# Who issues the weight loads, and who scales the last tile's gate, in a fused HGRN2 and pooling step on one core

## The reference

```
h = rmsnorm(x, norm_g);  z = h @ w_in          # q f i g_a u g_b m_a m_b
fgate = lb + (1 - lb) * sigmoid(f);  kin = 1 - fgate
o, S  = hgrn2(silu(q) * 128**-0.5, kin, i, log(fgate), S0)   # 4 heads of 128, chunks of 32
y_a = (rmsnorm(o) * silu(g_a)) @ w_proj_a
y_b = (mixed_pool(u) * pool_scale * silu(g_b)) @ w_proj_b
out = x + (sigmoid(m_a) * y_a + sigmoid(m_b) * y_b) @ w_out;  y = rmsnorm(out, final_norm_g)
```

## Time and profile before

| | us |
|---|---|
| median of 3 runs | 1368.67 |
| lowest, highest | 1368.1, 1369.56 |
| the profiled execution's own time | 1367.73 |
| its span, first to last instruction | 1366.0 |
| granted TensorE clock over the span | 0.999 |

### The profile page before, as it was taken

How to read it: one execution, slowest core, us unless ns; L and a number is a source line. 1 busy time by engine, 2 the same in 40 slices (tenths; PEclk the granted TensorE clock), 3 DMA queues, 4 the chain that set the end, 5 groups by cost and what they waited for, 6 DMA issues and landing times.

```text
span 1366.0 us, 21237 instructions
## 1 busy us (share of the span) xinstructions
PE 1351.6 (99%) x8236; PEld 1338.2 (98%) x8236; DVE 921.5 (67%) x1637; ACT 684.0 (50%) x994; POOL 248.6 (18%) x218
## 2 busy tenths in 40 slices
PE   9999999999999999999999999999999999999997
PEld 8999999999999999999999999999999999999997
DVE  8999655669974455698744467986545689974443
ACT  7556434355664344565643345665434456653332
POOL 3004131110132211101222020112310200140001
PEclk9999999999999999999999999999999999999999
DMA  6543633346526333565353335644433366634327
GB/s 219 152 129 123 217 117 115 115 122 206 148 94 223 123 108 109 147 179 149 113 204 122 108 124 152 174 134 151 167 122 108 125 175 200 177 112 172 122 95 81
DMA packets 140692, 195.92 MB, mean 143 GB/s; under 512 B 83760, under 2 KB 100656, under 8 KB 138928
## 3 DMA queue, kind: packets, MB, share of 16 engines
q1 hardware_dynamic: 140448, 194.54, 46.8%
q10 hardware_dynamic: 144, 0.01, 0.0%
HBM read 174.91 MB, written 19.61 MB: 142 GB/s over the span
## 4 chain that ended last, share of the span: by engine, by line
PE 86%; DVE 10%; DMA 1%; issue 1%; ACT 1%; SPq 0%; DVEq 0%; ACTq 0%
PE Z L551 27%; PE Z L553 27%; PE Z L552 27%; DVE wlo L1095 2%; PE B L604 1%; PE B L682 1%; PE B L672 1%; DVE h_b L1147 1%; DVE kj L1199 0%; DVE xres L1505 0%; DVE snew L1268 0%; DMA vtm<-v_blocks 0%; PE B L581 0%; DMA wraw<-w_all 0%; ACT hhi L1050 0%
## 5 line engine op out<-in xcount | busy, mean ns | idle before, releaser
L1095 DVE TENSOR_TENSOR wlo<-wraw,whi 128x1024 fp32r<-128x1024 f32 x278 | 362.8, 1305 | 306.5 <-ACT whi L823 306.5
L551 PE MATMUL Z<-hhi,whi 128*128 128x416 f32 x1576 | 552.5, 351 | 0.0
L553 PE MATMUL Z<-hhi,wlo 128*128 128x416 f32 x1576 | 549.3, 349 | 0.0
L552 PE MATMUL Z<-hlo,whi 128*128 128x416 f32 x1576 | 549.2, 348 | 0.0
L823 ACT ACTIVATE whi<-wraw 128x1024 fp32r<-128x1024 f32 x278 | 293.3, 1056 | 413.4 <-PE Z L553 412.3
L551 PEld LDWEIGHTS Z<-hhi,whi 128*128 128x128 f32 x1576 | 296.0, 188 | 0.9 <-issue 0.8
L552 PEld LDWEIGHTS Z<-hlo,whi 128*128 128x128 f32 x1576 | 296.0, 188 | 0.5
L553 PEld LDWEIGHTS Z<-hhi,wlo 128*128 128x128 f32 x1576 | 295.9, 188 | 0.3
L553 PE MATMUL Z<-mhi,wlo 128*128 128x416 f32 x320 | 112.3, 351 | 0.0
L552 PE MATMUL Z<-mlo,whi 128*128 128x416 f32 x320 | 111.8, 349 | 0.0
L551 PE MATMUL Z<-mhi,whi 128*128 128x416 f32 x320 | 111.5, 348 | 0.0
(11 more groups left out here) (243 smaller groups left out, 1642.0 us busy)
## 6 DMA issues: line engine op xcount, KB each, us to landing
wraw<-w_all SPq DMA_DIRECT2D x278, 512.0 KB, 3.5
xin<-xT SPq DMA_DIRECT2D x4, 1664.0 KB, 8.3
yT<-xres SPq DMA_DIRECT2D x4, 1664.0 KB, 8.5
xres<-xT SPq DMA_DIRECT2D x4, 1664.0 KB, 7.3
v_blocks<-h_vt SPq DMA_DIRECT2D x80, 52.0 KB, 3.1
vtm<-v_blocks SPq DMA_DIRECT2D x20, 192.0 KB, 3.9
ktm<-k_blocks SPq DMA_DIRECT2D x20, 192.0 KB, 3.5
k_blocks<-kt SPq DMA_DIRECT2D x64, 52.0 KB, 1.9
```

The costliest lines, as they stand in the source:

```text
L551: pe.matmul(out, wh, xh, start=first, stop=False)
L552: pe.matmul(out, wh, xl, start=False, stop=False)
L553: return pe.matmul(out, wl, xh, start=False, stop=final)
L1095: dve.tensor_tensor(wlo[n % RING][:], raw(t, n)[:], whi[n % RING][:].bitcast(F32), ALU.subtract).then_inc(wlo_made, 1)
```

## The change

Two things move to ScalarE. In tile 4 only, `kin` is made there from `sf` (one activation with a scale and a bias of one value for each partition), and the second half of `vms` is made there in slot 4h+8, as four activations of 96 x 128 scaled by a mask column each; the vector engine keeps the first half. The two halves get a semaphore each, and the clearing of `vms` goes (TensorE reads 96 rows only). In all tiles, from unit 12 of tile 0 on, ScalarE issues the loads of raw weights: at the end of its slot s it waits until `wlo` of unit s+2 is made, then issues the load of unit s+5 on its own DMA queue. SyncE keeps the loads of slots 3 to 11 of tile 0 and all other transfers.

```diff
+SYNC_LOADS = 12
 # SyncE
-                    if (s + RAW < NU or not last) and not (first(t) and (s + RAW < FIRST or s == 8)):
+                    if first(t) and FIRST <= s + RAW and s < SYNC_LOADS and s != 8:
                         weights(t, s)
 # SyncE, values_in
-                    sp.wait_ge(vms_made, 2 * h)
+                    for made in vms_made:
+                        sp.wait_ge(made, h)
 # TensorE
-                            pe.wait_ge(vms_made, 2 * h + 1)
+                            pe.wait_ge(vms_made[0], h + 1)
...
-                        pe.wait_ge(vms_made, 2 * h + 2)
+                        pe.wait_ge(vms_made[1], h + 1)
 # ScalarE
+            def weights(t, n):
+                act.wait_ge(wlo_made, nth(t, NU, n))
+                r = (t * NU + n) % RAW
+                act.dma_start(wraw[r][:], w_all[(n + RAW) % NU]).then_inc(w_landed[r], 16)
...
                         if s == 4 * h + 1:
                             sigmoid(t, "f", h, sf[h % 2], z_sem("f", h))
+                            if last:
+                                if h >= 2:
+                                    act.wait_ge(k_made, nth(t, 2 * H, 2 * (h - 2) + 1))
+                                else:
+                                    act.wait_ge(k_made, nth(t - 1, 2 * H, 2 * (h + 2) + 1))
+                                act.wait_ge(z_sem("f", h), z_done(t, "f", h))
+                                act.activation(kin[h % 2][:], sf[h % 2][:], ACT.Identity, bias=oml[:, h:h + 1],
+                                               scale=noml[:, h:h + 1]).then_inc(kin_made, 1)
...
+                        if s == 4 * h + 8 and last:
+                            act.wait_ge(split_v, 2 * h + 2)
+                            act.wait_ge(smasks, SMASKS)
+                            n = 3 * SAMPLE
+                            for b in range(4):
+                                ins = act.activation(vms[1][0:n, b, :], vs[h // 2][0:n].bitcast(F32), ACT.Copy,
+                                                     scale=bmask[0:n, 4 + b:5 + b])
+                            ins.then_inc(vms_made[1], 1)
...
+                if not (first(t) and s + 2 < SYNC_LOADS) and (s + 2 + RAW < NU or not last):
+                    weights(t, s + 2)
 # the vector engine
-                    if s == 2 and last:
-                        for v in vms:
-                            dve.memset(v[:].bitcast(F32), 0.0)
...
-                        if s == 4 * h + 1:
+                        if s == 4 * h + 1 and not last:
                             dve.wait_ge(z_sem("f", h), z_done(t, "f", h))
...
-                                for half in range(2):
-                                    dve.tensor_tensor(
-                                        vms[half][0:n], v[0:n].bitcast(F32).unsqueeze(1).broadcast_to([n, 4, P]),
-                                        bmask[0:n, 4 * half:4 * half + 4].unsqueeze(2).broadcast_to([n, 4, P]),
-                                        ALU.mult).then_inc(vms_made, 1)
+                                dve.tensor_tensor(
+                                    vms[0][0:n], v[0:n].bitcast(F32).unsqueeze(1).broadcast_to([n, 4, P]),
+                                    bmask[0:n, 0:4].unsqueeze(2).broadcast_to([n, 4, P]),
+                                    ALU.mult).then_inc(vms_made[0], 1)
```

More of the change, by code:

```diff
@@ L305, in step_kernel @@
         hist_kept, ybm_made, mlo_made = sem("hist_kept"), sem("ybm_made"), sem("mlo_made")
-        h32_made, hlo_made, y_made, vms_made = sem("h32_made"), sem("hlo_made"), sem("y_made"), sem("vms_made")
+        h32_made, hlo_made, y_made, vms_made = sem("h32_made"), sem("hlo_made"), sem("y_made"), [sem(f"vms_made{i}") for i in range(2)]
         lb_made, zeroed, ptmp_made = sem("lb_made"), sem("zeroed"), sem("ptmp_made")
```

## The result

The changed kernel takes 1373.0 us (median of six runs, 1371.97 to 1375.5), the kernel before, run beside it, 1368.8 us. The ratio is 1.0035 with a 95% interval of 1.0025 to 1.0044: slower by 4.2 us, by the medians, where 2.5 us less was forecast. The profiled execution is the slowest of the six: its own time is 1375.5 us for a span of 1373.8.

What follows compares the result with a forecast made beforehand. TensorE, busy 99% of the span, was taken as the bound, so only its waits could go: 2.3 us in tile 4 plus 0.4 in tile 0, less 0.2, is 2.5 off 1368.67, giving 1366.2 us; range 1365.0 to 1368.9.

Steps and rivals of the forecast that it cites:

- the loads, on SyncE's queue: In slot 4h+8, without the block's issue ahead of them, `vtm` and `ktm` are asked for 0.6 us earlier in every head.
- the slower rival: Late raw blocks make the scores miss TensorE in the heads of tiles 1 to 3: 1372.2 to 1374.7 us; chance 0.12.
- Tile 4 gives back 2.3 us: In tile 4's heads, relieving the vector engine removes TensorE's waits: 1.82 us idle plus 0.51 in matmul ends.
- 0.2 for ScalarE: Taken off the gain for ScalarE's new work showing in tile 4's thin margins; bounds nothing and 0.77 us.
- Tile 0 gives back 0.4: In tile 0, the earlier request for `ktm` covers TensorE's 0.38 us wait for it.
- ScalarE's new work: In tile 4, four `vms` instructions take 1.1 us and `kin` 0.52 to 0.65 per head, with 0.2 us showing.
- 265 issues at 0.35 us each: Load issues on ScalarE over all tiles: 93 us, hidden; `whi` to `whi` at a tile's end becomes 4.68 us.
- The new waits: 0: ScalarE's waits for `wlo` of unit s+2 cost 0; a block 1.7 us late stalls some tenths, within the margin.

Runs made afterwards that it cites:

- the block behind the trip: All loads on SyncE, gate and `vms` on ScalarE; against that kernel, slot 4h+8's block is issued behind the loads of `vtm` and `ktm`: 1366.03 us.
- the kernel with small blocks: The changed kernel, but each load ScalarE issues fetches only 64 of the block's 1024 columns: 1365.99 us, ratio 0.9982.
- the paced one: The changed kernel, but SyncE still waits for the `wlo` of each slot, though it issues no block there: 1377.56 us, ratio 1.0067.
- the block ahead of the stores: All loads on SyncE, gate and `vms` on ScalarE; against that kernel, slot 4h+8's block goes before the keys' stores in tiles 1 to 4: 1368.33 us.

## Why the prediction was wrong, by its steps

**The step that failed is "the loads, on SyncE's queue".** It said that `vtm` and `ktm` would be asked for 0.6 us earlier, since a block's issue of 0.47 us no longer stands ahead of them. `vtm` did come closer to the stores (2.14 us behind the first one, 2.52 before). `ktm` did not: its issue waits for the stores' landing, and that rose from 1.9 to 4.57 us. Even with the stores undisturbed, in the kernel with the block behind the trip, it was 3.30 us for 3.53, so 0.23 earlier and not 0.6: it goes out at 307.50, just as the last store has landed (307.49), and can't go earlier. I counted the removed issue and not what its place did: behind the stores on one queue, the block came after them. The price is 5.2 us of waits in tiles 1 to 3 of the profiled execution (1.97 + 1.13 + 0.91 + 0.76 + 0.44), in tiles that had no wait and therefore, in my sum, nothing to lose. I had put this term at nothing.

**The rule of the Trainium skill.** The rows show that transfers from the second queue lengthen those of the first (1.9 to 4.57 us). The Trainium skill, "DMA: Bandwidth & Descriptors", section "Issuing engines are not separate DMA queues", says that DMAs of several engines interleave on the same 16 engines; with that rule the trace agrees. I had drawn from it that transfers would be no faster and the sum unchanged; it also allows that a transfer gets slower once another queue has work, and that is what the runs show. The Trainium skill, section "Queues, rings and completion order" of the same page, has each DMA engine take turns between the queues it has work for. The 1.9 us with no block of another queue beside the stores and the 4.57 with blocks beside them fit that, and no run here shows the turns themselves.

**"The block for slot 4h+8 is asked for at the end of slot 4h+6, when the round trips have mostly landed"**, my argument against the slower rival, is refuted by the issue at 308.52: it goes out between the first store of the keys (307.02) and their landing (313.01). That rival (0.12, 1372.2 to 1374.7 us) had the sign, and the right cause at its root, blocks and round trips side by side; its path was another one, and that its size came out is luck (12 heads by 0.5 us in my sum, five waits of 0.4 to 2.0 us in the profile). It had the blocks late and the scores missed; in tiles 1 to 3 no score was late, and it was `ktm`, with a slack of 1.6 us that I hadn't worked out, and not the scores with their 3.0. I had priced the slack of the blocks and never that of the small transfers.

**Tile 4 gives back 2.3 us**: right in its mechanism, somewhat too large. The kernel with this part alone is 2.0 us faster (interval of the ratio 0.9977 to 0.9995), and its profile regains 1.9 us in tile 4. In the changed kernel 0.3, 0.3 and 1.1 us are regained at 1132, 1150 and 1166 us and 0.1 at the last wait, against the new wait of 0.46. Of that last wait 0.63 of the 0.77 us remain. I had relieved the vector engine by 2.8 us ahead of it; in the kernel with this part alone it comes to its last `vms` 1.8 us earlier (1185.69 for 1187.49). And what TensorE waits for there is the first half of `vms`, which stayed on the vector engine and took 1.29 us in both kernels, not the median's 0.68. The "0.2 for ScalarE" was too small for that wait.

**Tile 0 gives back 0.4**: no. The wait for `ktm` at 66 us goes in these kernels, but a wait behind it takes the time back: with the blocks on SyncE and the rest changed the lead is 0.44 us at 66 us and gone at 118.

**ScalarE's new work**: four instructions of 96 x 128 take 1.26 us in one group (1149.97), where I had 1.1; the Identity takes 0.74 for my 0.52 to 0.65, and no table is loaded for it. Small, but not wholly hidden: in the kernel without the moved loads the chain of waits runs through the four copies at 1163.99, and the vector engine stands 0.37 us for the log gate behind them, where it didn't before.

**265 issues at 0.35 us each**: 0.33 us each, but they cost nothing that shows: the kernel with small blocks has all of them. At the end of tile 0 `whi` follows `whi` in 4.34 us (269.39 to 273.73), 4.33 before, and not in my 4.68.

**"The new waits: 0"**: nearly true in tiles 1 to 4, not in tile 0, where ScalarE's own standing still delays the issue: 2.6 us and 1.6 of clock in one execution. In the run with the issue at the slot's start it is gone. Blocks are late in many slots, by 2.5 us in the mean where I had said 1.7 for one slot of most heads (30 waits of `whi`, 73.6 us in all; two before, 1.0 us), and nearly all of that is absorbed.

What stays open: the long stall in tile 0 hangs on one block's landing, 4.97 us in this profile; in the kernel with the loads alone and in the paced one the same block landed in 3.55 and 3.48, and the scores were late by 0.6. Why it varies no run shows, nor how much of the spread of the changed kernel (1371.97 to 1375.5 us) is due to it. The profile is one execution.

## What to carry to other kernels

When a large transfer is moved to another queue, look first at which small ones stood ahead of it on the old one: the line protected them. Work out the slack of every round trip through memory that overlaps the new place, from its landing to its user, and price it as stretched: here it grew by up to 3.9 us, from 7.5 to 11.5, in tile 2, head 1. A saved issue of 0.5 us is no gain if a wait for landing stands between it and the end; if the goal is only to relieve the issuing engine, keep the large loads off the stretches with round trips (1366.3 us with the heads' blocks on SyncE) or, on one queue, behind the trip (1366.03 us). The two can't be told apart, nor from all loads left on SyncE (1366.3 us). And a small transfer put behind another one's semaphore wait inherits that wait: 1.4 us in the kernel with the block ahead of the stores.

## What the hardware showed that I had not expected

- A DMA issue on ScalarE runs beside its activations and even ahead of them: one went out at 305.40 while the split of 305.34 ran, ahead of the table load and the sigmoid (306.40 and 307.69) that stand before it in the program. So "at the end of the slot" is not when it is issued here; the issue of 312.41, which went out 0.04 us behind the `wlo` that it waits for, is held by its wait.
- Four traces show TensorE at its lower clock level right after it stood still for 1.95 to 2.5 us (0.50 to 0.68 by window), which cost 1.5 to 1.6 us more each time. After 1.96 us of standing still at 318.13 the changed kernel kept the full clock, as this window shows, and so did the kernel with the loads alone after 2.1 us, and the paced one after 2.57 us at 1359.05, longer than any of the others. What tells these cases apart no run here shows.

```profile
318.10:320.00 1.90, 1.87 (x13) 1.87 (x14) 1.32 (x5) 0.97 (x2) 0.00 (x0) 1.00 0.22 36
```

- A block beside `ps_out` on the other queue (240 KB, in packets mostly under 512 bytes) took over 16 us to land, one beside `xres` (1.7 MB) 9.3; the median is 3.5. `ps_out` has a seventh of the bytes of `xres`.
- The read of the keys is faster without its usual neighbour on its own queue: 2.4 and 2.2 us (medians of its two parts) with the block behind the trip, 3.5 and 3.6 with the block ahead of it.
